# Two panels of the feed forward, w1 and w3, in seven products of quarters instead of eight

## What is computed

```python
h = rmsnorm_2(x, norm_ffn_g[l]) * (1.0 + sc2) + sh2
f = (jax.nn.silu(h @ ffn_w1[l]) * (h @ ffn_w3[l])) @ ffn_w2[l]
x = x + g2 * f
```

## Time and profile before

| | |
|---|---|
| median of 3 runs | 2512.34 us (2512.25 to 2516.28) |
| the profiled execution, span from its first to its last instruction | 2510.7 us |
| PE busy | 2441.7 us, 97% of the span, 14830 matmuls |
| DVE, ACT, POOL busy | 54%, 38%, 21% |
| DMA | 250.35 MB, mean 100 GB/s |

### The profile page before, as it was taken

One profiled execution on the slowest core, in us unless ns is written; L12 is line 12 of the kernel. 1 busy time (PEld: TensorE's weight loads), 2 busy tenths in 40 slices (PEclk: granted clock), 3 DMA queues, 4 the chain that ended last, 5 costly groups with the idle time before them and its releaser, 6 DMA issues.

```text
span 2510.7 us, 38214 instructions
## 1 busy us (share of the span) xinstructions
PE 2441.7 (97%) x14830; PEld 1984.7 (79%) x14830; DVE 1350.7 (54%) x2733; ACT 955.5 (38%) x1755; POOL 535.6 (21%) x527
## 2 busy tenths in 40 slices
PE   8999999999999999999999999999999999999998
PEld 6777878878887688788887668888888767888887
DVE  5567757665317654576728645333335844533333
ACT  5364264542324633554444334222225323422222
POOL 2112222122343122222474232000003241000001
PEclk9999999999999999999999999999999999999999
DMA  7302412124124034133533112323323212223322
GB/s 311 110 2 90 173 62 97 52 108 175 57 90 177 2 138 150 63 110 134 173 126 105 51 46 91 97 81 114 94 87 99 68 51 75 85 83 110 101 78 74
DMA packets 64642, 250.35 MB, mean 100 GB/s; under 512 B 7888, under 2 KB 10448, under 8 KB 54992
## 3 DMA queue, kind: packets, MB, share of 16 engines
q1 hardware_dynamic: 61216, 236.10, 27.6%
q0 software_dynamic: 2592, 11.54, 1.4%
q10 hardware_dynamic: 656, 0.30, 0.1%
HBM read 243.67 MB, written 4.19 MB: 99 GB/s over the span
## 4 chain that ended last, share of the span: by engine, by line
PE 83%; DVE 7%; ACT 4%; issue 3%; POOL 2%; DVEq 1%; ACTq 0%; DMA 0%; SPq 0%; POOLq 0%
PE ps L2617 34%; PE ps L2428 21%; PE ps L580 5%; PE ps L608 5%; PE ps L648 5%; PE ps L2594 4%; DVE ps L2006 2%; ACT probs L820 1%; PE ps L2407 1%; PE ps L2310 1%; POOL split_panels_first L1082 1%; PE ps L2562 1%; PE ps L2634 1%; PE ps L2449 1%; PE ps L2355 0%
## 5 line engine op out<-in xcount | busy, mean ns | idle before, releaser
L2617 PE MATMUL ps<-h_split,split_panels 128*128 128x512 f32 x2928 | 685.7, 393 | 1.8 <-ACT projected L1541 0.8
L2617 PEld LDWEIGHTS ps<-h_split,split_panels 128*128 128x128 f32 x2928 | 545.8, 188 | 127.0 <-issue 13.7
L2428 PE MATMUL ps<-h_split_first,split_panels_first 128*128 128x512 f32 (+1 forms) x2772 | 545.3, 354 | 4.7 <-POOL h_split_first L1114 1.9
L2428 PEld LDWEIGHTS ps<-h_split_first,split_panels_first 128*128 128x128 f32 x2772 | 445.3, 190 | 79.0 <-issue 8.6
L1951 DVE TENSOR_TENSOR split_panels<-panels,split_panels 128x1024 fp32r<-128x1024 f32 (+2 forms) x171 | 192.6, 1126 | 297.7 <-ACT split_panels L1277 293.9
L1082 POOL TENSOR_TENSOR split_panels_first<-panels_first,split_panels_first 128x1024 fp32r<-128x1024 f32 (+1 forms) x102 | 228.2, 2238 | 543.2 <-ACT split_panels_first L1269 543.2
L1277 ACT ACTIVATE split_panels<-panels 128x1024 fp32r<-128x1024 f32 (+2 forms) x210 | 204.2, 974 | 345.2 <-PE ps L2617 343.8
L1775 DVE SCALAR_TENSOR_TENSOR ps<-modulation_panels,silu_c,ps 128x256 f32<-128x256 f32 x480 | 225.2, 488 | 30.4 <-issue 2.1
L2617 PE MATMUL ps<-ffn_hidden_split,split_panels 128*128 128x512 f32 x990 | 225.0, 389 | 0.0
L2617 PEld LDWEIGHTS ps<-ffn_hidden_split,split_panels 128*128 128x128 f32 x990 | 185.8, 188 | 38.6
L1093 POOL TENSOR_TENSOR probs_turned<-probs_turned,probs 128x512 f32<-128x512 f32 x30 | 42.3, 1409 | 769.8 <-ACT probs L1484 769.8
(11 more groups left out here) (304 smaller groups left out, 2960.7 us busy)
## 6 DMA issues: line engine op xcount, KB each, us to landing
modulation_panels<-in_ada SPq DMA_DIRECT2D x64, 1024.0 KB, 4.9
panels<-in_w SPq DMA_DIRECT2D x88, 512.0 KB, 3.5
panels_first<-in_in SPq DMA_DIRECT2D x72, 512.0 KB, 5.9
panels<-in_in SPq DMA_DIRECT2D x42, 512.0 KB, 3.5
panels_first<-in_out SPq DMA_DIRECT2D x32, 384.0 KB, 3.0
panels<-in_w SPq DMA_DIRECT2D x32, 384.0 KB, 3.0
panels<-in_w SPq DMA_DIRECT2D x32, 320.0 KB, 2.8
panels<-in_out SPq DMA_DIRECT2D x16, 512.0 KB, 3.6
```

What stands on the lines that cost most here:

```text
L2428: ins = mm(at0, split1[:, s, w, c, :], hs1[:, h, c, lo:e], start=c == 0 and i == 0, stop=c == KC - 1 and i == 2)
L2617: ins = mm(out, split[:, n % SPLIT, a, c - base, :], moving(b, c), start=first and i == 0 and j == 0, stop=last and i == len(chunks) - 1 a ...
```

## The change

Write w1 and w3 of a hidden block as four quarters: w1 for the lower and the upper half of the inputs (chunks 0 to 3, 4 to 7), and w3 likewise; and h as four quarters: lower and upper inputs, first and second half of the tokens. The 8 products of quarters, 12 matmuls of 512 columns for the two token halves together (24 of 256), become 7 products of sums of quarters, each 4 chunks times 3 terms = 12 matmuls of 256 columns. This is done for the hidden blocks 2 to 21 of each layer (`PLAIN` = 2), so for 40 blocks in all. Blocks 0 and 1, w2 and all else are multiplied as before.

New work for it: in each layer, once, DVE makes four sums of quarters of h (`difference_of_halves`, `less`), ACT their high parts (`round_h_sum`), DVE two and POOL two of their low parts (`sum_lows`, `sum_rest`); the normed h is kept whole for this (`h_plain`, from `hm_at`). The last of the four is written over a quarter of `hs`, after block 1 has used it. For each block POOL makes four combinations of the weight quarters (`sum_weights`), one of them in place in the raw buffer of w3; ACT rounds seven weight parts instead of four, in four instructions, DVE makes their low parts in four. The seven products go into three banks (4 + k%2, 6 and 7), which hold running sums: between products ACT copies three intermediate states out (`take_first`, `take_second`, `take_third`) and DVE adds three halves of results (`first_half_of_h1`, `last_half_of_h3`, `last_half_of_h1`), and the bank is accumulated further afterwards. The slots of split_panels serve as the first six weight parts; the seventh has a tile of its own (split_last_sum).

Since these tiles share memory with tiles of the mixers, layer 1 sets three pads anew on POOL and loads the table counts again.

The core of the diff:

```diff
+            def seven_products(k, l):
+
+                s = block_no(k, l)
+                new = k == PLAIN
+                at_a, at_b, at_c = bank(4 + k % 2, 0, HS), bank(6, 0, HS), bank(7, 0, HS)
+                pe.wait_ge(f_ready, k - 1 + l * FFC)
+                pe.wait_ge(part_lo, 4 * s + 1)
+                quarter(at_a, w_parts[:, 0], corner(0, 0), True)
+                if s >= 1:
+
+                    pe.wait_ge(halves_summed, 3 * s - 2)
+                quarter(at_b, w_parts[:, 1], corner(1, 0), True)
+                pe.wait_ge(part_lo, 4 * s + 2)
+                pe.wait_ge(product_taken, 3 * s + 1)
+                if new:
+                    pe.wait_ge(h_summed, 6 * l + 6)
+                quarter(at_a, w_parts[:, 3], summed(1), False)
...
+                quarter(at_c, w_parts[:, 2], summed(0), True)
+                pe.wait_ge(part_lo, 4 * s + 4)
+                pe.wait_ge(product_taken, 3 * s + 2)
+                if new:
+                    pe.wait_ge(h_sum_rest, 2 * l + 1)
+                quarter(at_a, w_parts[:, 4], summed(2), False)
+                pe.wait_ge(product_taken, 3 * s + 3)
+                quarter(at_c, w_last, corner(1, 1), False)
+                pe.wait_ge(halves_summed, 3 * s + 2)
+                if new:
+                    pe.wait_ge(h_sum_rest, 2 * l + 2)
+                quarter(at_a, w_parts[:, 5], corner(0, 1), False)
```

```diff
+            def sum_weights(k, l):
+
+                n, s, q = w_panels(k), block_no(k, l), KC // 2 * P
+                one, three = raw[:, n % RAW, :], raw[:, (n + 1) % RAW, :]
...
+                if s >= 1:
+
+                    pool.wait_ge(part_lo, 4 * s - 2)
+                nc.gpsimd.tensor_tensor(w_sums[:, 0:q], three[:, 0:q], three[:, q:], ALU.add)
+                pool.drain()
+                nc.gpsimd.tensor_tensor(w_sums[:, q:2 * q], w_sums[:, 0:q], one[:, 0:q], ALU.subtract).then_inc(w_summed, 1)
+                nc.gpsimd.tensor_tensor(three[:, 0:q], three[:, 0:q], one[:, 0:q], ALU.subtract).then_inc(w_summed, 1)
+                pool.drain()
+                if s >= 1:
+                    pool.wait_ge(part_lo, 4 * s - 1)
+                nc.gpsimd.tensor_tensor(w_sums[:, 2 * q:3 * q], one[:, q:], w_sums[:, q:2 * q], ALU.subtract).then_inc(w_summed, 1)
```

```diff
+                    for k in range(first, end):
+                        take_first(k, l)
+                        round_difference(k, l)
+                        if (f, k) == (0, first):
+                            round_h_sum(3, l)
+                        if k + 1 < end:
+                            round_plain_parts(k + 1, l)
+                        else:
+                            round_panel(W2_AT[f], l)
+                        take_second(k, l)
+                        take_third(k, l)
+                        if k + 1 < end:
+                            round_first_sums(k + 1, l)
+                            round_last_sum(k + 1, l)
+                        else:
+                            round_panel(W2_AT[f] + 1, l)
+                        silu_of(k, l)
```

409 lines of the change are left out of this document (331 added, 78 removed).

## The result

The changed kernel takes 2568.5 us (median of 4 runs, 2564.5 to 2569.05) against 2512.81 us for the kernel before in the same session: a ratio of 1.0215, 95% interval 1.02 to 1.0229. It is slower by about 56 us, where 2497 had been forecast.

The account below looks back on a forecast made before the run. PE was taken to bound the kernel, busy 97% of the span. Shorter blocks (-33.6), layer starts (+17.6) and pads (+0.3) made -15.7 us, from 2512.3 to 2497 us; forecast case 2491 to 2505, range 2487 to 2512.

Parts of the forecast that it names:

- the starts of the layers: PE waits in the first blocks of each layer's feed forward: 8.8 us a layer, 17.6 for both, bounds 14.6 and 27.
- the pace: Distance of 256-column matmuls inside products: 0.1195 us, so 10.04 us a block for 10.88, 33.6 us saved over 40 blocks.
- R1: Rival: a fixed cost for each of 36 more matmuls per block takes the gain, time 2512 us; chance 0.08.
- R2: Rival: each of 280 products loses time at its wait, as weight loads cannot run ahead; 2517 us; chance 0.12.
- Whether the others hold this pace: Step on ACT, DVE, POOL and SP in each block: all deliver in time, smallest margins 0.65 to 0.8 us, cost nothing.
- the rest case: DVE slows by more than a quarter and falls behind in every block, 10.3 us or more each; 2507 us upwards; chance 0.05.
- A: Wait of PE at each layer's start for DVE's low part of w3 of block 1: 5.5 us, bounds 4.9 and 7.9.
- a bound for a slower DVE (a fifth): Upper bound of the wait for w3 of block 1: 7.9 us if DVE is a fifth slower (1.47 for 1.23).
- B: Wait of PE ahead of the third product of block 2, for DVE's rest_first_sums: 0.7 us, 0.5 to 1.1.
- C: Wait of PE ahead of block 2's seventh product, for a low part behind POOL's block 3 sums: 2.6 us, 1.9 to 4.5.
- The passages to w2 and back: Going over to w2 and returning to block 11: parts are made before use or nearly so, cost about nothing.
- The pads of layer 1: Three settings on POOL behind the norm in layer 1, with counts loaded long before use: 0.3 us.

Follow-up runs that it names:

- e1: Changed kernel with POOL's weight sums cut to one column in 18 of 20 blocks a layer (most sums left out): 2513.57 us, ratio 1.0006.
- e2: Changed kernel with each POOL weight sum replaced by three settings to zero, so POOL writes but reads nothing: 2517.8 us, ratio 1.0022.
- e12: Kernel before, without the change, plus four POOL subtractions of 512 columns in an unused buffer in blocks 2 to 21: 2512.78 us, ratio 1.0001.
- e10: e9 with block 2's weight sums and both sum_rest moved from POOL to DVE, less(3) behind hidden block 1: 2498.16 us, ratio 0.994.
- e4: Changed kernel with w2 parts of each layer's second half taking slots 1, 0, 2 in turn: 2557.54 us, ratio 1.0182.
- e9: Changed kernel with the edits of e3, e4 and e5 together: 2499.77 us, ratio 0.9953 to the kernel before.
- e5: Changed kernel with DVE making the weight sums of 18 of 20 blocks a layer, POOL only blocks 2 and 11: 2524.65 us, ratio 1.0042.
- e3: Changed kernel with w3 of block 1 split ahead of the later sums of h on DVE and ACT: 2544.86 us, ratio 1.0135.

## Why the prediction was wrong

Between the forecast for the span (-15.7 us) and the profiled execution (+52.0) lie 67.7 us. By the table above 38.0 of them are the gaps ahead of P5 and block 12, 21.5 the starts of the layers (39.1 for 17.6), 7.0 the rest and 1.2 the pace.

**The pace was right.** Inside a product the matmuls lie 0.120 us apart (0.1195 chosen), a block without gaps lasts 10.07 us (10.04), and over 40 blocks 32.4 us are saved (33.6). R1 and R2 are refuted: a wait that is met costs nothing, the distance at such a wait is 0.12 as well.

**The step that failed is in "Whether the others hold this pace": "I therefore cost all this at nothing".** Its list of DVE's durations came from rows during which POOL did nothing, and in the earlier trace rows POOL is at 0.00. Beside POOL's sums they do not hold: a DVE row with two operands in SBUF waits for the POOL row under way. Four such meetings, one of them the cast's, add 3.4 us to DVE's 7.2 (e1). Measured are 10.4 us of work, and with the hand-overs to and from the others 11.17 us per block instead of 10.07. This was the rest case, chance 0.05, "DVE falling behind in every block": it named the quarter beyond which the cover ends, and 3.4 of 7.2 is nearly a half. The Trainium skill, SBUF — State Buffer, Who interferes with whom, states this rule: a DVE instruction with two SBUF inputs contends with a GpSimd (POOL) instruction that reads SBUF, not with one that only writes; one in a mode with two ports contends with GpSimd in any case; the ports are an exclusive lock, and the loser is blocked fully. The traces agree: e1, e2 and e12 for the two inputs (0.69 beside settings, 1.64 beside sums), and the cast, which the page counts among the operations that can enter such a mode, is the only one that settings stretch (0.73). I had not weighed this rule, and it spoke against the change.

**A, forecast 5.5, was 9.6 us, and more behind it.** DVE's row for w3 was expected to end at 1563.9 and ended at 1568.7. The excess is in four rows: 2.29 and 2.31 for 1.23, 2.80 for 0.87, 1.82 for 0.43, together 5.5 us, less 0.6 for the earlier start. The first three ran beside `sum_weights(2)`, the fourth beside `sum_rest(2)`; e10, which has no POOL there, shows 1.23, 1.22 and 0.88, and e2, with settings there, shows them too, with A at 6.61 us. I had a bound for a slower DVE (a fifth), from one row, and did not ask why it was slow. The trace of the kernel before shows it. POOL was at work when that row started, at 1526.54:

```profile
1525.63 1.30 POOL L1093 TENSOR_TENSOR probs_turned<-probs_turned,probs 128x512 f32<-128x512 f32 x1 [4.22 <-ACT probs L1484]
```

POOL's row ends at 1526.93 and DVE's at 1528.01, 1.08 us later, just as in e12 (1607.30 and 1608.38). The same pair stands again 5.5 us on (POOL 1531.15 to 1532.45, DVE 1.48 us from 1532.05). So the price of the meeting could be read before the change was made: up to what is left of POOL's row, not a fifth.

Behind the wait PE had a granted clock of 0.50 for 4.0 us (mean 0.73 over the 24 matmuls), and they took 7.6 us in place of 5.7. I had not priced that.

**B was 0.4 to 0.5 us (forecast 0.7). C, forecast 2.6, was 4.8 us.** POOL's rows are held as well: 1.59, 2.10, 2.27 and 2.04 for the 1.41 that the prediction took, 10.6 us in all with the low part and the drains for 8.3. Behind it the granted clock was 0.56, near the level of 1.2 GHz, and 36 matmuls took 7.3 us for 4.5.

**The passages to w2 and back, put at "about nothing", were right where the prediction looked and missed the end of w2.** The last part of w2 in the second half landed in the slot that was freed last, 1.84 us of wait ahead of the last output, and again slower matmuls behind it (e4: 7.1 us in both layers by the traces). My working looked at the first parts of w2 and at the return to block 11 only.

The pads of layer 1 cost nothing that can be seen. With the three causes taken away e9 stands at 2500 us, 3 us from the forecast, and block 1 to block 4 take 39.5 us there, where the terms of the prediction make 39.8 (10.9 + 5.5 + 2 x 10.04 + 0.7 + 2.6). That the two sums agree is luck, not a proof of the prediction: e9's waits lie at other places (1.3, 3.8 and 0.9 us ahead of w3 of block 1, block 2 and its P7). What stays open: the gap of 2.9 us in block 12 goes with POOL's sums (e1, e5), and the chain above shows how, but it was not tried by itself; 7.3 us of the table is placed only roughly; and the 4 us between the change's profiled execution and its median have no place.

## What to carry to other kernels

When work goes to an idle engine, look at which operands it and its neighbour read, and take the neighbour's durations from a stretch in which both are at work; if there is none, price the neighbour's rows as own time plus the rest of the other's row (for the four rows of the steady block this is 0.14 us too much each). An engine that is nearly full turns any such stretch into a wait of PE in every block, and then order moves the wait while only removing work removes it: here DVE was better off doing POOL's sums itself. Price a wait of PE with the matmuls behind it: the clock had fallen behind the waits of 3.8 to 9.6 us (A, C and e3's). And before a gain is split among edits, compare the profiled executions as well as the medians: here they differ by as much as what looked like overlap.
